# Two blocks of a transformer on one core: the 64-row score matmuls of two heads or maps issued alternately

## What the reference computes

```python
# block 1: q, k, v of 8 heads of 64 for each attention, plus 8 index heads of 64
y_a = dilated_mixture(rope(qa), rope(ka), va)                    # "a"
dots  = einsum('bqhd,bsd->bqhs', qi_blk, ki)                     # index scores
score = einsum('bqh,bqhs->bqs', wi_blk, relu(dots)) * IDX_SCALE
_, sel = top_k(where(causal, score, -inf), 256)                  # keys that "b" may see
y_b = softmax(q_blk @ k[sel] * ATTN_SCALE) @ v[sel]              # "b"
x = x + merged @ w_out;  x = x + (silu(h @ w_gate) * (h @ w_up)) @ w_down
# block 2
s = einsum('bqhmd,bkhmd->bmhqk', q, k) * 64 ** -0.5 + bias       # "d": 4 heads, maps m = 0, 1 of 64
a = softmax(s[:, 0]) - lam * softmax(s[:, 1]);  o_d = a @ v
o_mla = softmax(q_m @ k_m * 192 ** -0.5) @ v_mla                 # "m": 4 heads of 128 + 64
x = x + concat([o_mla, o_d]) @ w_out;  x = x + square(relu(h @ w_up)) @ w_down
```

## Time and profile before

| | before |
|---|---|
| median of three runs | 3543.87 us |
| lowest, highest | 3529.85, 3552.47 us |
| span of the profiled execution | 3530.3 us |
| PE busy | 3256.4 us, 92% |
| vector engine busy | 1357.0 us, 38% |
| ScalarE, GpSimd busy | 947.8, 992.3 us |

### The profile page before, as it was taken

How to read it: one execution, slowest core, us unless ns; L and a number is a source line. 1 busy time by engine, 2 the same in 40 slices (tenths; PEclk the granted TensorE clock), 3 DMA queues, 4 the chain that set the end, 5 groups by cost and what they waited for, 6 DMA issues and landing times. The chain is left out here.

```text
span 3530.3 us, 36411 instructions
## 1 busy us (share of the span) xinstructions
PE 3256.4 (92%) x14286; PEld 2424.8 (69%) x14286; DVE 1357.0 (38%) x2077; ACT 947.8 (27%) x1344; POOL 992.3 (28%) x416
## 2 busy tenths in 40 slices
PE   5998988988899999999998998886999999999998
PEld 3556666766578788888876565463445788888887
DVE  4358888688632111111124444534333221212122
ACT  3233233223632211111123333432333211111110
POOL 4322331431034342342454000012000342424241
PEclk8988999989999999999999899898999999999999
DMA  6311111220051111111113001010001111111112
GB/s 161 90 36 42 54 48 30 61 59 31 1 190 49 48 48 48 48 48 54 43 42 110 13 29 32 4 33 24 6 0 60 48 48 48 52 43 54 42 53 66
DMA packets 261611, 176.20 MB, mean 50 GB/s; under 512 B 20660, under 2 KB 248884, under 8 KB 260916
## 3 DMA queue, kind: packets, MB, share of 16 engines
q1 hardware_dynamic: 261496, 174.64, 17.0%
HBM read 142.60 MB, written 25.20 MB: 48 GB/s over the span
## 5 line engine op out<-in xcount | busy, mean ns | idle before, releaser
L676 PE MATMUL big<-g_hi,w_hi 128*128 128x512 f32 x3328 | 1051.9, 398 | 33.1 <-POOL w_lo L1641 19.0
L676 PE MATMUL big<-g_lo,w_hi 128*128 128x512 f32 x3328 | 1038.0, 393 | 0.0
L676 PE MATMUL big<-g_hi,w_lo 128*128 128x512 f32 x3328 | 1035.8, 393 | 0.0
L676 PEld LDWEIGHTS big<-g_hi,w_hi 128*128 128x128 f32 x3328 | 631.8, 191 | 183.3 <-issue 32.7
L676 PEld LDWEIGHTS big<-g_lo,w_hi 128*128 128x128 f32 x3328 | 634.0, 190 | 135.6
L676 PEld LDWEIGHTS big<-g_hi,w_lo 128*128 128x128 f32 x3328 | 631.6, 190 | 134.5
L1641 POOL TENSOR_TENSOR w_lo<-w_raw,w_hi 128x1024 fp32r<-128x1024 f32 x99 | 242.4, 2448 | 1066.5 <-ACT w_hi L974 1066.5
L1719 POOL TENSOR_TENSOR w_lo<-w_raw,w_hi 128x1024 fp32r<-128x1024 f32 x76 | 181.9, 2393 | 64.2 <-ACT w_hi L1177 64.2
L1584 DVE TENSOR_TENSOR x_res<-big,x_res 128x1024 f32 x40 | 49.0, 1225 | 382.1 <-PE big L676 382.1
L1442 DVE MAX8 m<-idx_acc 128x8 f32<-128x384 f32 (+5 forms) x192 | 171.6, 894 | 21.7 <-POOL qb L1668 16.0
L1745 POOL TENSOR_TENSOR w_lo<-w_raw,w_hi 128x1024 fp32r<-128x1024 f32 x40 | 95.7, 2392 | 273.2 <-ACT w_hi L1205 273.2
(11 more groups left out here) (238 smaller groups left out, 3359.2 us busy)
## 6 DMA issues: line engine op xcount, KB each, us to landing
w_raw<-in_w_up SPq DMA_DIRECT2D x54, 512.0 KB, 3.9
w_raw<-in_w_in SPq DMA_DIRECT2D x51, 512.0 KB, 4.2
w_raw<-in_w_down SPq DMA_DIRECT2D x48, 512.0 KB, 4.0
w_raw<-in_w_gate SPq DMA_DIRECT2D x22, 512.0 KB, 3.7
rot<-rope_in SPq DMA_DIRECT2D x68, 128.0 KB, 2.3
x_res<-x_spill SPq DMA_DIRECT2D x2, 4096.0 KB, 14.6
w_raw<-in_w_out SPq DMA_DIRECT2D x16, 512.0 KB, 4.1
g_spill<-gst_a SPq DMA_DIRECT2D x9, 512.0 KB, 3.0
```

The costliest lines, as they stand in the source:

```text
L676: ins = pe.matmul(out[0:m, HALF * h:HALF * h + HALF], w[slot][:, col:col + m], x[:, HALF * h:HALF * h + HALF], start=(n == 0 and q == 0), ...
```

## The change

In the index stages the loops are turned: the row block is now outside and the head inside, and the matmuls of both heads are issued alternately, one of head 0 and one of head 1 for each stretch of 512 keys. ScalarE and the vector engine follow in the same order. In a, b and d the two heads or maps of a row block are made a pair and issued in the same way; m keeps its order. Both tiles of a pair are taken ahead of its first matmul.

```diff
@@ PE, index stage
-                for hh in range(2):
-                    for i in range(2, QT):
-                        key = ("idx", c, hh, i)
-                        out = take(key, s_arel)
-                        n1 = P * (i + 1)
-                        o = HD * hh
-                        for n0 in range(0, n1, HALF):
-                            ne = min(n0 + HALF, n1)
-                            ins = pe.matmul(out[:, n0:ne], ...)
-                        ins.then_inc(*s_big.mark(*key))
+                for i in range(2, QT):
+                    n1 = P * (i + 1)
+                    outs = [take(("idx", c, hh, i), s_arel) for hh in range(2)]
+                    for n0 in range(0, n1, HALF):
+                        ne = min(n0 + HALF, n1)
+                        for hh in range(2):
+                            o = HD * hh
+                            ins = pe.matmul(outs[hh][:, n0:ne], ...)
+                            if ne == n1:
+                                ins.then_inc(*s_big.mark("idx", c, hh, i))
@@ PE, scores of a, b, d and m
-                for ti, i in enumerate(st["tiles"]):
-                    for m, parts in enumerate(st["maps"](ti)):
-                        key = ("sc",) + s + (ti, m)
-                        out = take(key, s_rel)
...
+                pairs = [((ti, i, m, parts),) for ti, i in enumerate(st["tiles"]) for m, parts in enumerate(st["maps"](ti))]
+                if kind != "m":
+                    pairs = [pairs[0] + pairs[1]] + ([pairs[2] + pairs[3]] if kind == "d" else [])
+                for pair_ in pairs:
+                    outs = [take(("sc",) + s + (ti, m), s_rel) for ti, i, m, parts in pair_]
+                    n1 = keys(st, pair_[0][1])
+                    for n0 in range(0, n1, HALF):
+                        ne = min(n0 + HALF, n1)
+                        for out, (ti, i, m, parts) in zip(outs, pair_):
...
+                            if ne == n1:
+                                ins.then_inc(*s_big.mark("sc", *s, ti, m))
```

More of the change, by code:

```diff
@@ L787, in _ @@
                 pe.wait_ge(*s_dup.at("kiwi"))
-                for hh in range(2):
-                    for i in range(2, QT):
-                        key = ("idx", c, hh, i)
-                        out = take(key, s_arel)
-                        n1 = P * (i + 1)
-                        o = HD * hh
-                        for n0 in range(0, n1, HALF):
-                            ne = min(n0 + HALF, n1)
-                            ins = pe.matmul(out[:, n0:ne], qab[c % 2][o:o + HD, P * i:P * i + P], kib[o:o + HD, n0:ne],
+                for i in range(2, QT):
[5 more added lines that the diff above has]
+                            o = HD * hh
+                            ins = pe.matmul(outs[hh][:, n0:ne], qab[c % 2][o:o + HD, P * i:P * i + P], kib[o:o + HD, n0:ne],
                                             start=True, stop=True)
-                        ins.then_inc(*s_big.mark(*key))
+                            if ne == n1:
+                                ins.then_inc(*s_big.mark("idx", c, hh, i))
             elif stage == "gate":
@@ L812, in _ @@
                 }[kind]())
-                for ti, i in enumerate(st["tiles"]):
-                    for m, parts in enumerate(st["maps"](ti)):
-                        key = ("sc",) + s + (ti, m)
-                        out = take(key, s_rel)
-                        n1 = keys(st, i)
-                        for n0 in range(0, n1, HALF):
-                            ne = min(n0 + HALF, n1)
+                pairs = [((ti, i, m, parts),) for ti, i in enumerate(st["tiles"]) for m, parts in enumerate(st["maps"](ti))]
[7 more added lines that the diff above has]
+                        for out, (ti, i, m, parts) in zip(outs, pair_):
                             for q, (qa, ka) in enumerate(parts):
```

## The result

| | before | after |
|---|---|---|
| median, 20 runs each | 3542.63 us | 3553.11 us |
| lowest, highest | 3529.85, 3553.07 us | 3547.25, 3560.8 us |
| span of the profiled execution | 3530.3 us | 3547.9 us |

The ratio is 1.0032, with a 95% interval of 1.0022 to 1.0041: the change makes the kernel 11.3 us slower (8 to 15). That is within 1%, inside the range, and a third of the +34 us of the forecast.

What follows compares the result with a forecast made beforehand. The prediction took PE, busy for 92% of the span, to bound the kernel. Index stage +15, d +11 and a and b +8 made +34 us on the median 3543.87, giving 3578 us, with a range of 3548 to 3610.

Steps and rivals of the forecast that it cites:

- nothing here can get shorter: d steps: no pair ends earlier than its second map does today, so the bounds are 0 and 18 us.
- Index stage, +15: Four index stages: pairs wait for both of ScalarE's reads; 15 us longer, the middle of +1 and +29.
- 18.1 us at full clock: Each index stage after the change: PE work, reads, pair ends and first wait in series, 72.4 us for four.
- 4.1 and 5.9 us: Index stages before: time two stages lose to the fallen clock, leaving 65.3 of 75.3 us at full clock.
- the middle between +1 and +29: Index stages: +1 us if the clock stays full, +29 if it falls after two pairs; +15 taken.
- d steps, +11: Six of 16 d steps have reads starting 1.2 us later, 7 us, plus 4 for a fallen clock.
- 7.8 us or more: Sign of being right: six d steps grow from 6.6 us to this, first start to transposes.
- a and b, +8: a and b steps: ten of PE's waits for the vector engine grow by 0.8 us each; bounds 0 and 21.
- the clock falls wherever PE waits: Rival, whole kernel: index stage +29, d +18, a and b 8 to 21; +50 to +70 us, chance 0.18.
- the reads are hidden after all: Rival: clock stays full in the index stage, vector-engine shifts meet slack; +1 to +12 us, chance 0.23.
- the halves don't overlap in the new order: Rival: a pair costs two maps in a row in index, d, a and b; about 3710 us, chance 0.03.
- they run in series today: Rival: the changed matmuls run one at a time before, so alternation doubles their speed; about 3400 us, chance 0.04.

Runs made afterwards that it cites:

- E5: Kernel before, with both maps of d computed from the same half of the partitions; 33 us slower than before, ratio 1.0093.
- E8: Change in the index stages alone, plus five added products behind each pair but the last; 9 us faster than before, ratio 0.9975.
- E3: Kernel before with the change in the d steps alone; 2 us slower (-2 to +7), ratio 1.0006.
- E2: Kernel before with the change in the steps of a and b alone; 3.5 us slower (-2 to +8), ratio 1.0010.
- E1: Kernel before with the change in the index stages alone; 5.7 us slower (1.8 to 9.6), ratio 1.0016.

## Why the prediction was wrong in size

The sign and the mechanism were right: the halves already run side by side outside the index stage (eight starts in 1.4 us, E5), the pairs turn ScalarE's reads into idle time of PE, and the clock falls in it. The forecast was 34 us, 11.3 were measured. Two steps failed: what the kernel before loses to the clock in the index stage, taken as 10 us where the mean is 15, and "nothing here can get shorter" in d, where other stretches got shorter. By its steps:

- *Index stage, +15, measured +5.7.* The stage lengths were forecast as 18.1 us at full clock. E8, the only one that ran the pairs there at full clock, had 17.5, 18.5 and 17.5, and 20.7 at 0.92. Its added products are a little longer than the gaps of the small pairs (2.22 us from the first pair's start to the second's, against 1.93 after), so the sum of PE, reads and ends in series was right or up to 1 us too long. The step that failed is the baseline: "4.1 and 5.9 us" were taken as what before loses to the clock, from one execution in which two stages kept full clock. In the mean of four the same code has 80.5, which is 15 us over the 65.3 at full clock. That is 5.2 us of the error. Another 3.5 is the clock in the pairs: the change's stages came out at 86.8 in the mean, forecast 75.3 + 15 = 90.3, so the middle between +1 and +29 was a little high as well. The median hinted at the baseline: the profiled execution of after took 3549.7 us for a span of 3547.9, so a span of 3530.3 stands for a time of about 3532, some 10 us under the median of before, 3542.6. The forecast took its difference against that execution and added it to the median.
- *d steps, +11, measured +2 (-2 to +7).* The wait for both banks is there, 1.34 to 1.41 us, and in ten first pairs, not six (the 9.4 us on ScalarE's `rt_y` and the 4.2 on `dq` in the group by line). The clock falls in the second pair behind the product in one head and stays full in another, as shown above, so "7.8 us or more" from first start to transposes came out as 8.18 and 6.57. But "nothing here can get shorter" failed. The stretch from step 2 to step 3, both behind a norm, gets shorter, because PE stays at full clock in it. For the second head, before and then after:

```profile
2105.60:2125.90 20.30, 16.19 (x54) 8.72 (x53) 11.12 (x18) 9.79 (x15) 0.00 (x0) 0.87 0.00 1
```

```profile
2132.10:2150.50 18.40, 11.80 (x54) 6.72 (x54) 11.12 (x18) 9.78 (x16) 0.00 (x0) 1.00 0.00 0
```

20.3 us at a clock of 0.87 became 18.4 at 1.00. The two profiles with the change in d (after, E3) against the seven with d's code as before: from the first start of step 0 to that of step 1, the four heads together, it is 5.8 us longer (4.2 of it the wait ahead of step 1), from step 1 to 2 it is 9.4 longer, from 2 to 3 4.3 shorter, and from 3 to the next head 3.6 shorter. From the first start of the first step to that of the last it is 364.4 and 368.4 us, against 358.3 to 362.0 (mean 359.1). So d's own steps grew by 7, not far from the forecast but made up of other pieces. From the last step of d to the first score of m it is then 128.8 and 127.8 us, where the seven have 131.2 to 131.8, and m itself is 2 us shorter (below); d + m together are 773.2 and 776.1, against 770.0 to 775.7. Why the stretch behind d gets shorter is open.
- *a and b, +8, measured +3.5 (-2 to +8).* The size holds within the interval. The eight profiles without the change have a + b in 722.9 to 731.9 us (mean 726.9), the three with it 732.4, 734.0 and 736.1 (mean 734.2), 7 us more. The way was another one: the waits for normalised tiles grew only from 34.2 to 37.8 us instead of by the whole shift in ten steps, and a larger part is the waits ahead of the pairs (26 us more idle time in the two groups, 25 less busy).
- *The rivals.* That the clock falls wherever PE waits was right for all four index stages, but the time was not: before already loses 15 us of clock there in the mean, and that can't be lost again. That the reads are hidden after all (+1 to +12) gave the right time for a reason that the traces exclude, 31.0 us of idle time on ScalarE's reads. That the halves don't overlap in the new order, and that they run in series today, are excluded by the undisturbed pair and by E5. The 3.0 us that the prediction sets against the 1.4 are those of a pair wholly in series; starts strictly in the order of the program, with both halves free to work, would give 6 x 0.43 = 2.6, which the 1.4 excludes as well. The 64.6 us of the index stage, too, are reads and PE in series, which the joint wait makes, and not what follows from reads being the bound.
- *m and what follows it.* m wasn't to change; between its first and last score matmul, and from its last value product to the end, after is 2.2 and 4.1 us shorter. The second stretch takes 813.8 to 818.0 us in the eleven profiles, all with the same code there, so nothing is drawn from it. m itself came out 2.2 us shorter in E2 and E3 too; a stage that the change doesn't touch with another length was named as a sign of being wrong, and this one is not settled.

## What to carry to other kernels

Two 64-row maps in different halves of the array overlap when they stand next to each other in the program and each has its bank; they need no instruction-by-instruction alternation. Give each its own wait: a joint wait turned the reader's time into idle time of TensorE, and of the 22 us between the two ways of waiting here about 15 were the clock that fell in it. And where a clock term is in the sum, the profile of one execution is one sample: compare its time with the median before taking a difference from it.

## What the hardware showed that I had not expected

- In the first stage of after, the fourth pair already ran at the lower clock level, after three pairs of 0.92 to 1.35 us with gaps of 1.0 to 1.4 us between them. A hundred added instructions in such gaps (E8 against E1) kept the clock at its upper level in three stages and made the kernel 15 us faster.
- With both maps in one half, the order before lost 33 us and the alternated one 115 us: the overlap in d is worth more than the change moves in all. A pair of eight 512-column instructions takes 3.1 us from first to last start in one half and 1.4 in two.
- The same instructions in the same order took from 75.3 to 83.9 us in the index stages; length times granted clock, summed over the four stages, is about 65 us in all four executions.
